# The rope key's 64-column tile of an input projection, computed for two pieces of tokens side by side in TensorE's columns

## The reference

```
z = x @ lp['w_in']
u_a, g_a, u_b, g_b, c_q, c_kv, k_r, g_c = jnp.split(z, SPLIT_IDX, axis=-1)
...
kr = _rope(k_r[:, :, None, :], pos)[:, :, 0]
```

## Time and profile before

| | |
|---|---|
| median of 3 runs | 2236.63 us (2236.17 to 2240.82) |
| span of the profiled execution | 2378.0 us |
| time of the profiled execution beside its span | none is given by the page |
| TensorE busy (matmul) | 2170.7 us, 91% |
| VectorE, ScalarE, GpSimd busy | 1077.5, 682.4, 226.2 us |
| mean granted TensorE clock | 0.937 of full |

### The profile page before, as it was taken

How to read it: one execution, slowest core, us unless ns; L and a number is a source line. 1 busy time by engine, 2 the same in 40 slices (tenths; PEclk the granted TensorE clock), 3 DMA queues, 4 the chain that set the end, 5 groups by cost and what they waited for, 6 DMA issues and landing times. The chain is left out here.

```text
span 2378.0 us, 55745 instructions
## 1 busy us (share of the span) xinstructions
PE 2170.7 (91%) x24578; PEld 1400.4 (59%) x24578; DVE 1077.5 (45%) x2577; ACT 682.4 (29%) x1853; POOL 226.2 (10%) x225
## 2 busy tenths in 40 slices
PE   8999899997899988999989998899888999899998
PEld 4655577774565655664456555777645656556543
DVE  2034157764565444443320331677636644444433
ACT  1231144442454411110012311444425543111100
POOL 0000000010000132202100000010000001222022
PEclk9999988987999988899999999999979998888999
DMA  5110000000003154442111101000000032544321
GB/s 186 45 59 22 36 3 4 4 4 20 1 1 80 45 220 170 171 152 71 59 55 45 58 22 36 3 4 4 4 20 1 1 81 75 196 171 167 108 71 64
DMA packets 49843, 150.85 MB, mean 63 GB/s; under 512 B 15106, under 2 KB 19458, under 8 KB 40132
## 3 DMA queue, kind: packets, MB, share of 16 engines
q1 hardware_dynamic: 37316, 71.79, 9.2%
q0 software_dynamic: 12288, 75.51, 8.7%
HBM read 129.70 MB, written 12.86 MB: 60 GB/s over the span
## 5 line engine op out<-in xcount | busy, mean ns | idle before, releaser
L373 PE MATMUL psum<-work 128*128 128x368 f32 (+1 forms) x1632 | 514.1, 477 | 9.2 <-DMA work<-w_z 6.8
L373 PEld LDWEIGHTS psum<-work 128*128 128x128 f32 (+1 forms) x1632 | 307.4, 189 | 212.3 <-issue 25.7
L2191 PE MATMUL psum<-work,mixed 128*128 128x512 f32 (+1 forms) x576 | 248.8, 592 | 1.6 <-PEq L1863 1.6
L2191 PEld LDWEIGHTS psum<-work,mixed 128*128 128x128 f32 (+1 forms) x576 | 106.2, 186 | 137.7 <-issue 137.7
L1932 PE MATMUL psum<-work,ub 32*64 32x256 f32 x2048 | 145.9, 443 | 39.9 <-issue 35.7
L2059 DVE STREAM_TRANSPOSE work<-work 128x1024 f32<-128x1024 f32 x128 | 150.5, 1214 | 0.4 <-issue 0.3
L1635 ACT ACTIVATE work<-psum,work 128x128 f32<-128x128 f32 (+8 forms) x130 | 97.8, 752 | 157.0 <-DVE work L1738 155.4
L1519 PE MATMUL psum<-work 96*128 96x512 f32 (+3 forms) x384 | 139.2, 496 | 3.7 <-ACT work L1635 2.1
L1803 POOL DMA_INDIRECT work<-cache_ckv,pages x64 | 60.6, 948 | 757.8 <-PE psum L1469 386.0
L2069 DVE TENSOR_REDUCE work<-psum 128x1 f32<-128x1024 f32 x32 | 39.2, 1225 | 205.5 <-PE psum L1932 205.5
L1932 PEld LDWEIGHTS psum<-work,ub 32*64 32x64 f32 x2048 | 71.5, 148 | 97.9 <-issue 91.6
(11 more groups left out here) (260 smaller groups left out, 3270.2 us busy)
## 6 DMA issues: line engine op xcount, KB each, us to landing
work<-w_z SPq DMA_DIRECT2D x4, 2560.0 KB, 11.3
work<-w_out SPq DMA_DIRECT2D x4, 2048.0 KB, 9.3
xres<-work SPq DMA_DIRECT2D x16, 512.0 KB, 2.9
work<-xT SPq DMA_DIRECT2D x4, 1104.0 KB, 8.9
work<-x_tok SPq DMA_DIRECT2D x8, 512.0 KB, 4.1
work<-xres SPq DMA_DIRECT2D x8, 512.0 KB, 4.3
work<-w_z SPq DMA_DIRECT2D x1, 2304.0 KB, 12.4
o_ckv<-ckv SPq DMA_DIRECT2D x2, 1104.0 KB, 4.3
```

What stands on the lines that cost most here:

```text
L373: return nc.tensor.matmul(zb[i % 2][n][rows, 0:G], z_weights(m, g)[:, k, lo:lo + Z_W[i]], xT[:, k, span(n)], start=k == 0, stop=k == DK - 1)
L2191: last = nc.tensor.matmul(yb[t % 2][half][0:n, :], m.mixed[:, k, lo:lo + n], wo[half][:, k, :], start=k == 0, stop=k == DK - 1)
```

## The change

The key's tile gets a function of its own. Tokens are cut into 4 pieces of 276 instead of 3 of 368. Pieces 0 and 1 are accumulated in one bank, piece 0 in partitions 0 to 63, piece 1 in partitions 64 to 127, alternating for each slice of the contraction; pieces 2 and 3 follow in a second bank. ScalarE evacuates four pieces, all to partitions 64 to 127 of `kr`, of which pieces 0 and 2 come from partitions 0 to 63.

```diff
+KR_G = T // 4
...
             def product(i, n, k):
...
-                rows = slice(64, P) if Z_TILES[i] == "kr" else slice(0, P)
-                return nc.tensor.matmul(zb[i % 2][n][rows, 0:G], z_weights(m, g)[:, k, lo:lo + Z_W[i]],
+                return nc.tensor.matmul(zb[i % 2][n][:, 0:G], z_weights(m, g)[:, k, lo:lo + Z_W[i]],
                                         xT[:, k, span(n)], start=k == 0, stop=k == DK - 1)
+
+            def rope_key(i):
+
+                g = max(j for j in range(N_ZL) if Z_LOADS[j] <= i)
+                lo = Z_AT[i] - Z_AT[Z_LOADS[g]]
+                for pair in range(2):
+                    for k in range(DK):
+                        for half in range(2):
+                            n = 2 * pair + half
+                            last = nc.tensor.matmul(zb[i % 2][pair][64 * half:64 * half + 64, 0:KR_G],
+                                                    z_weights(m, g)[:, k, lo:lo + Z_W[i]],
+                                                    xT[:, k, n * KR_G:(n + 1) * KR_G], start=k == 0, stop=k == DK - 1)
+                return last
...
-                    for n in range(NG):
+                    if Z_TILES[i] == "kr":
+                        last = rope_key(i)
+                    for n in range(NG if Z_TILES[i] != "kr" else 0):
                         for k in range(DK):
                             last = product(i, n, k)
                     last.then_inc(s_z, 1)
...
-                    for n in range(NG):
+                    for n in range(4 if name == "kr" else 0):
+                        last = nc.scalar.copy(kr[64:P, n * KR_G:(n + 1) * KR_G],
+                                              bank[n // 2][64 * (n % 2):64 * (n % 2) + 64, 0:KR_G])
+                    for n in range(NG if name != "kr" else 0):
...
-                        elif name == "kr":
-                            last = nc.scalar.copy(kr[64:P, span(n)], bank[n][64:P, 0:G])
```

## The result

The changed kernel takes 2222.22 us in the median of 4 runs (2217.3 to 2229.69); the kernel before, beside it, 2236.4 (2232.9 to 2240.82, 4 runs). The ratio is 0.993, with a 95% interval of 0.99 to 0.9959. In five further rounds it was 0.993 again, with 0.9906 to 0.9954. The forecast was 2221.8 us, in a range from 2217 to 2229, and a ratio of 0.9934.

What follows compares the result with a forecast made beforehand. The prediction took TensorE's stream to bound the key's tile and the projection. Pairs at the price of one save 7.41 us a layer, 14.8 in both, nothing given back: 2236.63 us becomes 2221.8, range 2217 to 2229.

Steps and rivals of the forecast that it cites:

- The bound: Key's tile in the input projection: bound by TensorE's stream, nothing waits; 14.98 us a layer, a product every 0.309 us.
- The price of a pair: Key's tile: two products side by side run in the time of one, 0.232 us; tile 7.57 us instead of 14.98.
- The evacuation: ScalarE's copies of the key: four of 276 tokens take about 1.3 us instead of 1.19, costed at nothing.
- The cover: The copies' bank is wanted only a whole tile (14.8 us) later, hiding their extra 0.1 us.
- Who must follow: Other engines and weight loads around the key's tile follow 7.4 us earlier; nothing of the gain is given back.
- The sum: Whole kernel: 14.8 us off both layers; profiled span 2363.2 us, median 2221.8 us.
- Rival 1: Key's tile: packing pays in part, 0.06 us more a pair; tile 9.5 us, 11 us gained, 2225.6 us; chance 6%.
- rival 3: Key's tile: each product's weight load is exposed; tile 23.6 us, 8.7 us a layer lost, 2254 us; chance 3%.
- Rival 2: Key's tile: the two halves do not overlap at all; 14.85 us, no gain, 2236.6 us; chance 4%.
- Rival 4: Stages after the projection: gain is made but clock dips fall elsewhere, some 4 us either way; full pairs with scatter 87%.
- The scatter: Same code in two layers differs by 2.6 us, some 4 for two; about 4.5 us can be told from none.

Runs made afterwards that it cites:

- first trace of before: First profile of the kernel before, no edit: span 2378.0 us against a median of 2236.63 us; the new trace has 2237.4 us.
- kernel with one pair: Against the changed kernel: groups of 368 tokens again, the first two side by side, the third alone; tile 10.04 us, ratio to before 0.9937.
- two second traces: New profiles, no edit, of the kernel before (span 2237.4 us) and of the changed kernel.
- pairs of 69 tokens: Against the changed kernel: each 276-token piece cut into four of 69, still in pairs; tile 7.83 us, ratio to before 0.9911.
- halves in turn: Against the changed kernel: eight slices of one half first, then those of the other; tile 12.40 us, ratio to before 0.9973.
- four side by side: Against the changed kernel: only the key's 32 columns multiplied, four 276-token pieces at once, exchanged copy by two transfers; tile 3.86 us, ratio to before 0.9893.

## Why the prediction was right

**The bound.** Right. The tile was bound by its stream, TensorE set the length of the projection, and doubling the tile (15.03 us) brought the projection back to the length of before.

**The price of a pair.** Right to 0.001 us: 0.2326 measured, 0.232 forecast from the pitch of the tile itself and L1963. The row that decided was the one closest in form: same shape of weights, same bank, 256 columns. The tile came out at 7.59 us for a forecast of 7.57. The Trainium skill (TensorE: Matmul & The Clock Gate, Part 3, under "Measured speedup vs the span model") has 2.38x for three side by side, which by the prediction's estimate would have given 9.5 us. The runs gave 1.97x for two and, with 32 columns, 3.9x for four, entry and exit included: that ratio does not carry over to this stream.

**The evacuation.** Mis-sized, and it did not matter. Four copies take 1.56 us and not 1.3. Each copy has a length between the two rows from which I had it, 0.38, but they no longer overlap: in the first trace of before three copies of 0.46 us fill 1.19, one each 0.365; here four of 0.38 fill 1.56, one each 0.39. The kernel with one pair has three copies of 368 tokens again and takes longer than before, in ScalarE's timeline:

```profile
48.82 1.40 ACT L447 COPY kr<-psum 64x368 f32<-64x368 f32 x3 [8.77 <-PE psum L384]
```

A step there is 0.47 us where before it was 0.365, so a copy out of other partitions than the one ahead of it costs 0.1 us more. A change of bank is not the cause: the copies of before each read another bank and overlap. The cover held: the bank is wanted 15 us later.

**Who must follow.** Right. The gate's products, the latent copies and the waits at L413 all moved by 7.5 us and grew by nothing; no load of weights came late. The end of the projection in layer 1 was to come 14.8 us earlier. Between the two second traces it comes 21.0 us earlier (1400.60 and 1379.60), of which 9.1 and 7.4 are the projections and 4.4 is the stage between them, whose code did not change.

**The sum.** 14.8 us forecast; 14.2 in the first comparison, and 0.7% of 2242 us, 15.7, in the second (the medians alone, 2242.03 and 2223.33, are 18.7 apart). That the first median came within 0.4 us of the forecast is luck: its four runs lie 12.4 us apart. What is not luck is the tile, 7.39 us shorter for a forecast of 7.41.

**The rivals.** Rival 1 fell with the single pair (10.04 us and not 11.0), rival 3 with the pairs of 69 tokens. Both had leaned on the earlier trace rows, and those rows came from the disturbed trace: in the new one the eight tiles of L1932 pay in full (0.215 us for eight), where the prediction read 3.4 times and not 8. There was a warning that I left alone: a profiled span 6% above the median says that some stage is not as it is in the timed runs. I said that the stage of the change was not the one, which was right, and then took evidence from a stage that was. Rival 2 did not come about, but the run with halves in turn was meant to act it out and did so only in part: at each change of half the other half began while records of the first still waited. Rival 4 came about as scatter: the stages behind moved by some 4 us each between traces.

**The scatter.** Too small. I took 2.6 us a layer from one trace's two layers, and the three runs' 4.65 us as what a measurement can tell. 30 runs of before in one session spread from 2226.0 to 2252.1 us, and the intervals of the ratios are 0.002 to 0.003 wide on either side. A gain of 0.7% is clear of that; one of 0.2% would not have been.

## What to carry to other kernels

In these float32 streams a product with 64 or 32 weight columns costs what a full one costs, and a second beside it in other output partitions (with 32 columns, three more) is free if neighbours in the program go to different halves: look for a loop of that form already in the kernel, its pitch is the price. Before copying a layout that duplicates columns for convenience, ask what the duplicates cost in the array; here it was half of the paired tile (7.59 against 3.86 us). And when a profiled span is far from the timed median, find the stage that holds the difference before taking any row as evidence.

## What the runs showed of the hardware that was not expected

- TensorE behaves as if it kept a queue for each half of its columns: one record running and three waiting (or one product and one, which no run here separates), counted in records or products and not in time (12.08 us for blocks of 16 records with 276 columns and the same with 138). Once the last record of a block is in its half's queue, work for the other half starts ahead of those that still wait. In all kernels here the product that carries the signal, the last of the tile, also ends last; where the other half's queue could outlast it, no run here tried it.
- The first record in a half that stood idle takes 0.05 us more (halves in turn: 0.447 us in place of 0.396, and the next one starts 0.284 us after it in place of 0.2325); one that is fed does not.
- A load of 64 columns of weights is recorded with 0.137 us, yet 256 of them went by in 7.9 us beside the streams, one each 0.062 us in each half. The recorded length is not the spacing at which loads can follow each other.
- ScalarE's copies from PSUM overlap by 0.1 us if they leave from the same partitions as the one before (0.46 us long, one each 0.365), and not if they change (0.46 long, one each 0.47, with one pair; 0.38 long, one each 0.39, with four side by side). The runs do not tell whether the change of source does it, or that some of these copies go to other partitions than they come from.
